# A two-layer mixer network: two groups of the second layer's input projection are made token tile by token tile inside the first layer's closing stage

## The reference, cut to what matters

```
out = einsum('tef,efd->td', hid * combine, w_down)       # mixture of experts: each token adds two expert rows
x   = _layer_norm(ALPHA*x + gate*out, ln_g, ln_b)        # end of layer 0
h   = x * (1.0 + scale) + shift                          # layer 1, modulation
bg, cg, xv, ga, gb = split(h @ w_in, CD_SPLITS)          # layer 1, first projection: 1024 -> 2560
y_sc = bg * _dwconv(cg * xv, sc_w)                       # 3 taps
u = _layer_norm(_dwconv(ga*sigmoid(gb), cf_w) + cf_b)    # 31 taps
y = concatenate([y_sc, silu(u)]) @ w_out
```

## Time and profile before

| | |
|---|---|
| runs | 1370.72 us median of 3 (1369.12, 1370.72, 1376.93) |
| profiled execution | 1368.97 us, of which the span of the trace is 1367.2 |
| PE busy in the span | 1222.3 us (89%) |
| DVE, ACT, POOL busy | 589.5, 344.3, 187.8 us (43%, 25%, 14%) |
| mean granted clock of PE | 0.962 of full |

### The profile page before, as it was taken

One profiled execution on the slowest core, in us unless ns is written; L12 is line 12 of the kernel. 1 busy time (PEld: TensorE's weight loads), 2 busy tenths in 40 slices (PEclk: granted clock), 3 DMA queues, 4 the chain that ended last, 5 costly groups with the idle time before them and its releaser, 6 DMA issues.

```text
span 1367.2 us, 17311 instructions
## 1 busy us (share of the span) xinstructions
PE 1222.3 (89%) x6677; PEld 690.5 (51%) x6677; DVE 589.5 (43%) x1171; ACT 344.3 (25%) x687; POOL 187.8 (14%) x177
## 2 busy tenths in 40 slices
PE   4999999999999998998987877999999999977774
PEld 2554455545446675555644433555554565644442
DVE  2123332400346666755322216069986773411217
ACT  1334444410224524111111106011033121211112
POOL 1000000010000010311252121600000402441210
PEclk9999999999999999998999998999999999999997
DMA  9414568745010227008799948111113147999864
GB/s 345 181 42 149 186 204 292 266 178 186 7 66 9 70 90 277 31 32 308 292 410 408 410 179 314 36 62 62 63 62 154 47 154 274 409 409 408 314 233 182
DMA packets 98369, 266.60 MB, mean 195 GB/s; under 512 B 12571, under 2 KB 14882, under 8 KB 97138
## 3 DMA queue, kind: packets, MB, share of 16 engines
q1 hardware_dynamic: 81888, 228.26, 44.3%
q0 software_dynamic: 16080, 37.14, 7.4%
q10 hardware_dynamic: 322, 0.12, 0.0%
HBM read 257.65 MB, written 28.79 MB: 210 GB/s over the span
## 4 chain that ended last, share of the span: by engine, by line
PE 67%; SPq 13%; DMA 8%; DVE 6%; issue 3%; ACT 3%; ACTq 0%; POOLq 0%; DVEq 0%; POOL 0%
PE ps L2129 18%; PE ps L2140 15%; SPq L661 4%; PE ps L2598 4%; SPq L662 4%; SPq L660 4%; DMA weights<-in_moe_w_up 3%; PE ps L2048 3%; PE ps L2265 3%; PE ps L2427 2%; PE ps L2615 2%; PE ps L2232 2%; PE ps L2408 2%; PE ps L2502 1%; PE ps L2100 1%
## 5 line engine op out<-in xcount | busy, mean ns | idle before, releaser
L2129 PE MATMUL ps<-h_cm,weights 128*128 128x512 f32 (+1 forms) x896 | 245.7, 436 | 1.2 <-ACT h_cm L985 1.2
L2129 PEld LDWEIGHTS ps<-h_cm,weights 128*128 128x128 f32 x896 | 136.5, 192 | 114.1 <-issue 113.8
L2140 PE MATMUL ps<-weights,mix_cm 128*128 128x512 f32 x288 | 126.2, 595 | 1.1 <-ACT mix_cm L1171 1.1
L2598 PE MATMUL ps<-weights,scratch 128*64 128x256 f32 x704 | 96.4, 434 | 28.2 <-DMA weights<-in_moe_w_up 26.4
L1660 DVE SCALAR_TENSOR_TENSOR scratch<-scratch,taps_cm 128x655 f32<-128x655 f32 x120 | 101.5, 897 | 2.5 <-ACT scratch L1242 1.0
L2598 PEld LDWEIGHTS ps<-weights,scratch 128*64 128x64 f32 x704 | 61.5, 157 | 67.5 <-issue 30.9
L2140 PE MATMUL ps<-weights,h_cm 128*128 128x512 f32 (+1 forms) x240 | 83.8, 508 | 4.0 <-DMA weights<-in_ab_w_in 4.0
L2140 PEld LDWEIGHTS ps<-weights,mix_cm 128*128 128x128 f32 x288 | 53.9, 190 | 65.0 <-issue 64.9
L1952 DVE TENSOR_TENSOR scratch<-ps,scratch 128x128 f32<-128x128 f32 x38 | 11.1, 292 | 173.9 <-ACT scratch L1280 155.7
L2140 PEld LDWEIGHTS ps<-weights,h_cm 128*128 128x128 f32 x240 | 42.6, 195 | 45.0 <-issue 40.8
L844 POOL DMA_INDIRECT expert_rows<-scratch,gather_scatter_rows x32 | 33.0, 1032 | 188.2 <-ACT scratch L1286 101.1
(11 more groups left out here) (415 smaller groups left out, 1912.4 us busy)
## 6 DMA issues: line engine op xcount, KB each, us to landing
weights<-in_mod_w SPq DMA_DIRECT2D x13, 2048.0 KB, 8.7
weights<-in_moe_w_gate SPq DMA_DIRECT2D x44, 512.0 KB, 9.3
weights<-in_moe_w_up SPq DMA_DIRECT2D x44, 512.0 KB, 13.5
weights<-in_moe_w_down SPq DMA_DIRECT2D x44, 512.0 KB, 15.3
x_tm<-in_mod_w SPq DMA_DIRECT2D x10, 2048.0 KB, 8.6
weights<-in_ab_w_in SPq DMA_DIRECT2D x6, 2048.0 KB, 13.0
weights<-in_cd_w_in SPq DMA_DIRECT2D x5, 2048.0 KB, 20.2
h_cm<-in_moe_w_gate SPq DMA_DIRECT2D x16, 512.0 KB
```

Of the source, the lines that this page charges most:

```text
L2129: ins = T.matmul(ps(*name)[:, a:b], w[:, k, col:col + 128], HT[:, k, a:b], start=(k == 0), stop=(k == KD - 1))
L2140: ins = T.matmul(ps(*name)[:, at:at + w.shape[2]], src[:, k, t * 128:t * 128 + 128], w[:, k, :], start=(k == 0), stop=(k == KD - 1))
L2598: ins = T.matmul(pair_bank(u)[SL * i:SL * i + SL, 0:256].rearrange("p (g f) -> p g f", g=2), XGT[:, u % 2, at:at + SL], w[:, k, :, :], sta ...
```

## The change

The first two groups of the projection, `("cd", 3, 0)` and `("cd", 3, 1)`, leave the loop of layer 1. They are made inside the combination, in ten pieces of one token tile each: eight matmuls with 128 columns, as soon as ACT has moved that tile to `HT`. The slots of the combination are no longer dealt in turn but written down: `("slot", s)` says which slot the next group takes. The new order of PE is ys0, ys1, ys2, xT0, ys3, xT1, piece (0, tile 0), ys4, xT2, pieces (0, 1), (1, 0), (1, 1), xT3, pieces (0, 2), (1, 2), xT4, pieces (0, 3), (1, 3), (0, 4), (1, 4), where the first number is the group. By the new slots ys0, ys2, ys4 and xT4 share slot 0, all of xT0 to xT3 share slot 1, the two early groups hold slots 2 and 3, and ys1 and ys3 use slot 3 before.

```diff
+EARLY_CD = [(CD_ORDER[0], j) for j in range(2)]
-COMBINE_ORDER = [[("ys", 0), ("ys", 1), ("ys", 2), ("xT", 0), ("ys", 3), ("xT", 1), ("ys", 4), ("xT", 2), ("xT", 3), ("xT", 4)],
+COMBINE_ORDER = [[("slot", 0), ("ys", 0), ("slot", 3), ("ys", 1), ("ys", 2), ("xT", 0), ("slot", 3), ("ys", 3), ("slot", 1), ("xT", 1),
+                  ("cd", 0, 0), ("slot", 0), ("ys", 4), ("xT", 2), ("cd", 0, 1), ("slot", 3), ("cd", 1, 0), ("cd", 1, 1),
+                  ("slot", 1), ("xT", 3), ("cd", 0, 2), ("cd", 1, 2), ("slot", 0), ("xT", 4), ("cd", 0, 3), ("cd", 1, 3),
+                  ("cd", 0, 4), ("cd", 1, 4), ("slot", 1)],
                  [("ys", t) for t in range(NT)]]
...
         def open_group(pe, *name):
...
-            n = GROUP[name]
-            if n >= 4:
-                pe.wait_ge(slot_free[n % 4], n // 4)
+            slot, uses = GROUP[name]
+            at_least(pe, slot_free[slot], uses)
...
+            def early_projection(i, t):
+
+                name = ("cd",) + EARLY_CD[i]
+                w = w8(weights(pe, "cd", EARLY_CD[i][0]))
+                col = 128 * EARLY_CD[i][1]
+                if t == 0:
+                    open_group(pe, *name)
+                emptied(pe, "xT", 1, t)
+                if t == 4:
+                    pe.wait_ge(h_half, NT + 1)
+                for k in range(KD):
+                    ins = T.matmul(ps(*name)[:, t * 128:t * 128 + 128], w[:, k, col:col + 128], HT[:, k, t * 128:t * 128 + 128],
+                                   start=(k == 0), stop=(k == KD - 1))
+                if t == 4:
+                    close_group(ins, *name)
...
                         for j in range(4):
-                            project_cm(("cd", c, j), w, j * 128)
+                            if (c, j) not in EARLY_CD:
+                                project_cm(("cd", c, j), w, j * 128)
```

More of the change, by code:

```diff
@@ L200, in psum_groups @@
                 for j in range(4):
-                    g += [("cd", c, j)] + CD_BEHIND.get((c, j), [])
+                    if (c, j) not in EARLY_CD:
+                        g += [("cd", c, j)] + CD_BEHIND.get((c, j), [])
         for kind, t in OUT_ORDER:
@@ L207, in psum_groups @@
         g += [("clock", l, 0), ("ct", l), ("clock", l, 1), ("tb", l), ("clock", l, 2)]
-        g += [(kind, 1 if kind == "xT" else l, t) for kind, t in COMBINE_ORDER[l]]
-    return {name: n for n, name in enumerate(g)}
+        for kind, *at in COMBINE_ORDER[l]:
+            if kind == "slot":
+                g.append((kind, *at))
+            elif kind != "cd":
+                g.append((kind, 1 if kind == "xT" else l, at[0]))
+            elif at[1] == 0:
+                g.append(("cd",) + EARLY_CD[at[0]])
+    where, used, slot = {}, [0] * 4, 0
+    for name in g:
+        if name[0] == "slot":
+            slot = name[1]
+            continue
+        where[name] = (slot, used[slot])
+        used[slot] += 1
+        slot = (slot + 1) % 4
+    return where
 def build(nc, A, O):
@@ L336, in ps @@
                 return bank(3)
-            return PS[:, GROUP[name] % 4, :]
+            return PS[:, GROUP[name][0], :]
         def open_group(pe, *name):
@@ L342, in open_group @@
                 return
-            n = GROUP[name]
-            if n >= 4:
-                pe.wait_ge(slot_free[n % 4], n // 4)
+            slot, uses = GROUP[name]
+            at_least(pe, slot_free[slot], uses)
         def close_group(ins, *name):
-            ins.then_inc(fill_full if name in FILL else slot_full[GROUP[name] % 4], 1)
+            ins.then_inc(fill_full if name in FILL else slot_full[GROUP[name][0]], 1)
         def filled(eng, *name):
@@ L353, in filled @@
             else:
-                eng.wait_ge(slot_full[GROUP[name] % 4], GROUP[name] // 4 + 1)
+                eng.wait_ge(slot_full[GROUP[name][0]], GROUP[name][1] + 1)
         def release(ins, *name):
-            ins.then_inc(fill_free if name in FILL else slot_free[GROUP[name] % 4], 1)
+            ins.then_inc(fill_free if name in FILL else slot_free[GROUP[name][0]], 1)
         def emptied(eng, *name):
@@ L362, in emptied @@
             else:
-                eng.wait_ge(slot_free[GROUP[name] % 4], GROUP[name] // 4 + 1)
+                eng.wait_ge(slot_free[GROUP[name][0]], GROUP[name][1] + 1)
         def bank(b):
@@ L2110, in x_turn1 @@
                 close_group(ins, "xT", 1, t)
+            def early_projection(i, t):
[12 more added lines that the diff above has]
+                    close_group(ins, *name)
             def combine(l):
                 pe.wait_ge(pair_diag, 2 * NT * (l + 1))
-                for kind, t in COMBINE_ORDER[l]:
-                    if kind == "ys":
+                for kind, *at in COMBINE_ORDER[l]:
+                    t = at[0]
+                    if kind == "slot":
+                        continue
+                    if kind == "cd":
+                        early_projection(*at)
+                    elif kind == "ys":
                         mixed_sum(l, t)
```

## The result

The changed kernel took 1359.99 us (median of 9 runs, 1358.1 to 1365.66) beside 1370.72 for the kernel before (9 runs, 1365.69 to 1376.93): ratio 0.9922, 95% interval 0.9898 to 0.9946, 10.7 us faster. The forecast was 1364.4 in a range from 1361.3 to 1368.3. The sign was right, the gain nearly twice the forecast's 5.7, and the time lies 1.3 us under the range. Compared twice more, the same kernel took 1363.48 and 1364.00 us, ratios 0.9952 (0.9933 to 0.9971) and 0.9963 (0.9940 to 0.9987): 6.6 and 5.1 us, and both times inside the range. The mean of the three is 0.9946, or 7.4 us.

What follows compares the result with a forecast made beforehand. PE bounds the end behind 851.28. Of 19.07 us removed, 7.39 is gained after returned pieces and late sum, less 1.68 for clock: 5.7. Middle of 1363.3 and 1365.0, rounded up: 1364.4 us, range 1361.3 to 1368.3.

Steps and rivals of the forecast that it cites:

- The price of a piece: Each early projection piece on PE takes 1.79 us, its weight loads hidden; splitting costs 0.3 us a group.
- The rival in which they set the price: Unhidden weight loads make each early piece on PE 3.07 us: 6.1 us slower, chance 0.03.
- The late sum: In the combination, ys4 starts DVE 4.41 us late; 4.01 us reaches ACT's norm of tile 3 without a clock fall.
- The clock in the hole: PE's new 2.46 us idle time before tile 1's turn lets the clock fall, costing 1.68 us.
- The rest is mainly the low clock at their start: 1.65 us: The two removed groups took 19.07 us, 17.30 at full clock; low clock at the projection's start lost 1.65.
- The range: Whole execution: 1361.3 to 1368.3 us, from the forecast, the first rival, rival 2 and part of rival 3.
- the first rival: The clock doesn't fall in PE's new hole before tile 1's turn: gain 7.4 us, chance 0.27.
- 2: Chunk 3's weights land 4 us later, so pieces and ys4 wait: gain 3.2 us, chance 0.08.
- part of 3: Rival 3: gain given back behind, DVE's taps keeping 3.2 us or layer 1's expert loads leaving 0; chance 0.08.
- the rival in which the taps take it back: DVE's taps don't start earlier, so PE waits 2.5 us at the mean, 3.2 us left; in rival 3, chance 0.08.
- The weights for the early pieces: Chunk 3's weights land at 836.2, needed at 837.7: 1.5 us of cover, no wait on PE.

Runs made afterwards that it cites:

- the one with one group: Changed kernel with only the first early group, the second back in layer 1's loop: ratio 0.9996 to the kernel before, 39.68 us from first turn to second drain.
- the slots alone: Changed kernel's new slots kept, both early groups back in layer 1's loop: ratio 1.0001 to the kernel before, 44.54 us from first turn to second drain.
- the piece moved: Changed kernel with piece (0, 0) put behind the last expert sum and tile 2's turn: ratio 0.9952 to the kernel before.
- the filled hole: Changed kernel with three matmuls of unread result on PE ahead of tile 1's turn: 1359.37 us, ratio 0.9928 to the kernel before.
- that sum first: Changed kernel with the last expert sum (ys4) directly behind ys3, ahead of tile 1's turn, run twice: 1360.43 and 1359.56 us, ratios 0.9937 and 0.9918.

## Why the prediction was right in its steps and wrong in its range

*The price of a piece: right.* Four pieces are 64 records in 7.31 us in the timeline above; (7.31 - 0.275) / 63 = 0.112 each, 1.79 a piece. The durations of the pieces' line in the changed kernel (shortest, median, longest in ns):

```profile
L2141 PEld LDWEIGHTS ps<-h_cm,weights x160: 190/192/337, 834.9 to 861.2; 128*128 128x128 f32 x160
L2141 PE MATMUL ps<-h_cm,weights x160: 275/275/421, 835.1 to 861.3; 128*128 128x128 f32 x160
```

The weight loads last 0.19 us and follow each other at 0.112, hidden. The rival in which they set the price, and the rule of the Trainium skill ("TensorE: Matmul & The Clock Gate", "Part 3: Packing small matmuls — row/col tiling") that speaks for it, don't hold for this shape. The same section also lets a load run ahead when it goes to a background weight buffer; whether that is what happens here no row shows.

*The late sum: right.* Without a fall the norm of tile 3 was to come 4.01 us late, with it 5.69. It comes 844.74 - 826.74 = 18.00 us behind the first turn, and came 842.17 - 829.86 = 12.31 behind it: 5.69.

*The clock in the hole: the price right, the certainty not.* 1.64 us measured. But behind the same hole of 2.53 or 2.54 us it fell in three of six profiles (both of the first two of the changed kernel and the one with one group; not in the third of the changed kernel, with the slots alone, or with the piece moved). "Since the hole lies between two that brought a fall, I take 1.68" was not borne out. Nor need it be a coin toss. In the three profiles in which the clock fell in the hole, it had also fallen some 20 us earlier, behind the wait for the expert rows: the first four records of the first sum took 3.06, 3.35 and 2.60 us. In the three in which it stayed up they took 1.96. The rows of the changed kernel, first and third profile:

```profile
813.11 3.06 PE L2118 MATMUL ps<-mix_cm,mod_parts 128*128 128x512 f32 x4 [2.49 <-DMA scratch<-expert_rows]
...
821.50 1.96 PE L2118 MATMUL ps<-mix_cm,mod_parts 128*128 128x512 f32 x4 [2.57 <-DMA scratch<-expert_rows]
```

The profile with the filled hole had the fall at the first sum too (3.19 us) and none behind the filler. Six profiles show the two together; what links them was not tested.

*"The rest is mainly the low clock at their start: 1.65 us": mis-sized.* This came from one execution. In the other profile of the kernel before it was 3.0 us, and the two groups took 20.5. On the yardstick the change gives 41.14 (mean of two) less 34.33 (mean of three), 6.8 us, where the forecast took one profile's 5.7. The difference is this term (0.65 on average) and the fall taken as certain (0.54): both made the forecast too small. 6.8 agrees with the 7.4 of the three comparisons.

*The range: this is the step that failed.* The base was not the miss: 1364.4 is 5.7 us under 1370.1, and the kernel before measured 1370.72. But "The forecast and the first rival hold from 1361.6 to 1365.0; with 2 and part of 3 the range is 1361.3 to 1368.3" is made of the bounds of the mechanisms alone, around a sum from one profile. It puts at nothing, without a reason, what executions differ by outside the stage. The runs showed in its place that this is some 4 us: 10.7 us were measured in the first comparison, where the stage gives 6.8, and 6.6 and 5.1 in the other two. That the later medians of 1363.48 and 1364.00 fall near 1364.4 is partly luck as well, since the forecast's gain was 1.1 us too small.

Where the differences lie can be read from the twelve profiles, most of which differ in no instruction outside the combination. The first sum starts anywhere from 811.86 to 821.50 us. From the second drain to the column sums it is then 138.25 or 138.26 us in every one, and 26.13 or 26.14 on to the second projection: what the stage gains is kept to 0.01 us, so the rival in which the taps take it back is out. From the start of the second projection to the end of the span it is 330.5 to 337.0 us. In four of the twelve the first 32 records of layer 1's expert products took 5.36 to 6.33 us, at a fallen clock, and 3.67 in the other eight; these four have the four longest ends, 334.6 to 337.0. The rest of the spread, and that ahead of the first sum, has no cause shown. That the differences average out rests on three comparisons.

*The weights for the early pieces: right.* No profile shows PE waiting for them.

## What to carry to other kernels

Moving work into another engine's waiting time pays for the part that leaves the end, less what the move delays on the way there. Look for the instruction whose lateness is queued in front of two engines (here one sum), and put the moved work and any newly shared buffer behind it: the same pieces with that sum first gave 10 us on the stage instead of 7, though the times of whole executions don't yet tell the two versions apart. And measure a gain of half a per cent inside the stage, between two instructions of one profile, before comparing medians: the yardstick repeated to 0.02 us where the clock did the same, the medians to 4.

## What the runs showed of the hardware

An idle time of 2.54 us on PE decides nothing by itself: with the same instructions around it the granted clock fell to 0.50 in two profiles and stayed at 1.00 in a third. Behind the wait before the first expert sum, 2.48 to 2.66 us long, it fell in seven of the twelve profiles, in one after 2.49 us and not in another after 2.66. In the expert stages, too, the length of the wait alone doesn't tell. Waits of 2.75 and 3.88 us for weights (changed kernel, layer 1) were followed by 32 gate and up records in 3.67 us, at the full clock, and waits of 2.29 and 2.71 us (kernel before, layer 1) by 32 such records in 5.36. Dense 128-column float32 matmuls ran with weight loads of 0.19 us starting every 0.112 us, so that the loads overlap one another as well as the matmuls.
